# A decoder block on one core: attention and its output projection in one block of code, the projection's chunks in the order 2 3 0 1 6 4 5 7

## Chip, cores and metric

One core of a Trainium2 chip runs the whole kernel. The metric is the device time of one execution in microseconds (us). The kernel before took 1774.89 us (median of three runs, 1772.11 to 1775.58).

## What is computed

A decoder block for 1024 tokens of width 1024. The part that matters here is the attention branch and its output projection:

```
u = rms_norm(x, g_mix)
xr, gr, q, k, v, fl, m_lru, m_attn = split(u @ w_in)
y_lru  = (rg_lru(conv(xr)) * gelu(gr)) @ w_lru_out
o      = forgetting_attention(q, k, v, log_sigmoid(fl + b_forget))   # 8 heads of 128
y_attn = o @ w_attn_out
x = x + (sigmoid(m_lru) * y_lru + sigmoid(m_attn) * y_attn) @ w_out
x = x + hierarchical_moe(rms_norm(x, g_ffn), ...)
return rms_norm(x, g_final)
```

## The kernel before

The program is a row of nine stages (`write`): input norm, first value products, halved input products, LRU values, LRU output projection (`branch_out(0)`), attention (`attention`), attention output projection (`branch_out(1)`), merge projection with routing, experts. Each stage is a block with one instruction stream for each engine. `stage` ends each with a clearing of the stage's semaphores and a barrier of all engines, so no engine starts a stage before all have finished the last one.

All large products are made of float32r matmuls in three parts. An operand is split into a high part (ScalarE, ACT below, copies it to float32r) and a low part (VectorE, DVE below, subtracts that copy from the original); a product is high times high, high times low and low times high. `product` (L204) does this for one 128-row output tile of 1024 tokens: for each of the 8 chunks k of the inner dimension it issues six matmuls of 512 columns, 48 in all. Its argument `chunks_in` makes TensorE (PE) wait for each chunk's low part first.

**Attention.** Each of 8 heads goes through 8 score tiles of 128 queries, from the longest to the shortest: scores on PE (L1395), bias and minimum on DVE (L1492), exponent on ACT (L1444), turn on PE (L1404), high and low part of the turned tile on ACT and DVE (L1438, L1467), and, for each half of the queries, the product with the values on PE (`values`, L1419), which counts up `pv_mm`. The second half of the queries (g = 1, values product over 8 key blocks) comes first, then the first half (g = 0, 4 key blocks). DVE multiplies each half by the inverse sums (`output`, L1476), and SyncE (SP) stores it to `o_d` in DRAM (`store`, L1323). Result chunk k is head k: `o_d[k]`, 128 rows by 1024 tokens. The last `values` of the last head is the 16th, and so is its `output`.

**Between the two stages.** At the end of `attention`, SP issues the loads of chunks 0 to 3 from `o_d` into the four staging tiles `ao_in0` to `ao_in3` (L1359), behind the store of head 7's second half and ahead of the store of head 7's first half. SP's queue is in program order: every wait in it holds what stands behind it.

**Output projection.** `branch_out(1)` has chunks 4 to 7 loaded by SP into the same four staging tiles (L1148), each once the low part of the chunk that was there is made. ACT copies each chunk's high part to `uh` (L1187), DVE makes the low part in `ul` (L1205), PE runs `product` for four tile columns in each of two passes (L213). In the first of the eight products PE waits chunk by chunk. DVE gates each product with `ao_sg` (L1223), adds it to `mix` (L1226), and the result is split again (L1192, L1211). SP's loads of `ao_sg` (L1153) stand behind the chunk loads, ACT's split of the second weight block (L193) behind the eight chunk copies. The weights of the first pass are loaded long before.

The memory of `uh` and `ul` overlays that of attention: chunks 0 and 1 of `uh` lie where the first half's turned tiles (`at_pth0`) are, chunks 2 to 5 on the second half's (`at_pth1`), 6 and 7 on `at_ptl0`; chunks 0 to 3 of `ul` lie on `at_ptl1`. The staging tiles overlay the query and key tile of even heads.

Of the kernel before, what the change touches and what calls it, by code (L numbers as in the profile page):

```python
# [21 lines left out]


# [3 lines left out]
F32 = mybir.dt.float32  # L27
# [12 lines left out]
NH = 8  # L40
# [20 lines left out]
BANKS = 6  # L61
VALUE_USE = (0, 0, 1 + D // WB, 1 + D // WB)
# [7 lines left out]
SLOTS = (NE + MAXX) * BLK  # L70

# [30 lines left out]
class Kernel:  # L102
# [101 lines left out]
    def product(self, pe, ps, s, c, chunks_in=None, by_half=False):  # L204

        wh, wl = (w[s][:, :, c * P:(c + 1) * P] for w in (self.w_h, self.w_l))
        for half, k in ((half, k) for half in range(2 if by_half else 1) for k in range(KD)):
            if chunks_in is not None and half == (1 if by_half else 0):
                pe.wait_ge(chunks_in, k + 1)
            for w, u, first, last in ((wh, self.uh, k == 0, False), (wh, self.ul, False, False),  # L210
                                      (wl, self.uh, False, k == KD - 1)):
# [896 lines left out]
    def branch_out(self, branch):  # L1108
# [22 lines left out]
        in_hi, in_lo, own = (self.sem(f"{tag}_{n}") for n in ("hi", "split", "own"))  # L1131
        mix_hi, mix_lo = self.sem(f"{tag}_mix_hi"), self.sem(f"{tag}_mix_lo")
        both = [(s, c) for s in range(2) for c in range(2)]
        source = lambda k: k_.mix[:, k, :] if branch == 0 else stage[k % 4][:, :]
        new = slice(HALF if branch == 0 else 0, T)

        with nc.Block() as block:
            @block.sync
            def _(sp):
                if branch == 0:  # L1140
                    for q in range(4):
                        sp.wait_ge(k_.quad_stored[q], 16 * k_.quads_until(NBLOCKS))
# [7 lines left out]
                def gates(i):  # L1150
                    for s, c in both:
                        sp.wait_ge(gated[s][c], i)
                        sp.dma_start(sg[s][c][:, :], k_.sig_d[branch, 4 * i + 2 * s + c]).then_inc(loaded[s][c], 16)  # L1153
                with sp.Fori(0, n_pairs - 1) as i:
                    gates(i)
                    for s in range(2):
                        k_.load_block(sp, s, p0 + i + 1, k_.w_block(weights, WB * (2 + s) + 2 * WB * i))
                gates(n_pairs - 1)
                if branch == 0:

                    for c in range(2):
                        sp.wait_ge(k_.v_stored[c], 32 * D // WB * NT // 4)
                    sp.wait_ge(k_.bias_stored, 16)
                    for c in range(2):
                        if c == 0:
                            k_.load_head_qk(sp, 0, c)
                            k_.load_head_bias(sp, 0, c)
                        k_.load_head_v(sp, 0, c)
                for s in range(2):
                    k_.load_block(sp, s, p0 + n_pairs, k_.w_block(following, WB * s))  # L1170

            @block.tensor
            def _(pe):
                with pe.Fori(0, n_pairs) as i:
                    for s, c in both:
                        if c == 0:
                            pe.wait_ge(k_.w_lo[s], p0 + i + 1)
                        pe.wait_ge(gated[s][c], i)
                        k_.product(pe, k_.ps[2 * s + c], s, c, in_lo if (s, c) == (0, 0) else None, branch == 0 and (s, c) == (0, 0))\
                            .then_inc((k_.w_first, k_.w_used)[c][s], 1)  # L1180

            @block.scalar
            def _(act):
# [4 lines left out]
                def mixed_high(i, s, c):  # L1188
                    if branch == 1 and (i, s, c) != (n_pairs - 1, 1, 1):
                        n = 4 * i + 2 * s + c  # L1190
                        act.wait_ge(gated[s][c], i + 1)
                        act.activation(k_.mix_h[:, n, :], k_.mix[:, n, :], ACT.Copy).then_inc(mix_hi, 1)  # L1192
                for i in range(n_pairs):
                    k_.split_hi(act, 1, p0 + i)
                    for c in range(2):
                        mixed_high(i, 0, c)
                    k_.split_hi(act, 0, p0 + i + 1)
                    for c in range(2):
                        mixed_high(i, 1, c)

            @block.vector
            def _(dve):
                for k in range(KD):
                    dve.wait_ge(in_hi, k + 1)
                    dve.tensor_tensor(k_.ul[:, k, new], source(k)[:, new], k_.uh[:, k, new].bitcast(F32),  # L1205
                                      ALU.subtract).then_inc(in_lo, 1)
                def mixed_low(i, s, c):
                    if branch == 1 and (i, s, c) != (n_pairs - 1, 1, 1):
                        n = 4 * i + 2 * s + c
                        dve.wait_ge(mix_hi, n + 1)  # L1210
                        dve.tensor_tensor(k_.mix_l[:, n, :], k_.mix[:, n, :], k_.mix_h[:, n, :].bitcast(F32),  # L1211
                                          ALU.subtract).then_inc(mix_lo, 1)
                for i in range(n_pairs):
                    k_.split_lo(dve, 1, p0 + i)
                    for s, c in both:
                        dve.wait_ge((k_.w_first, k_.w_used)[c][s], p0 + i + 1)
                        dve.wait_ge(loaded[s][c], 16 * (i + 1))
                        mix = k_.mix[:, bass.ds(4 * i + 2 * s + c, 1), :].rearrange("p a t -> p (a t)")
                        if branch == 0:
                            dve.tensor_tensor(mix, k_.ps[2 * s + c][:, :], sg[s][c][:, :], ALU.mult)\  # L1220
                                .then_inc(gated[s][c], 1)
                        else:
                            dve.tensor_tensor(sg[s][c][:, :], k_.ps[2 * s + c][:, :], sg[s][c][:, :], ALU.mult)\  # L1223
                                .then_inc(own, 1)
                            dve.wait_ge(own, 4 * i + 2 * s + c + 1)
                            dve.tensor_tensor(mix, mix, sg[s][c][:, :], ALU.add).then_inc(gated[s][c], 1)  # L1226
                        mixed_low(i, s, c)
                        if (s, c) == (0, 1):
                            k_.split_lo(dve, 0, p0 + i + 1)
# [18 lines left out]
    def load_head_v(self, eng, i, c):  # L1248
        for part in range(2):
            eng.dma_start(self.at_v[c][:, part, :, :].bitcast(F32),  # L1250
                          self.v_d[i, part, :, :, c * HD:(c + 1) * HD]).then_inc(self.v_in[c], 16)

    def attention(self):
# [23 lines left out]
        inv_stored, inv_in = ([sem(f"at_inv_{n}{g}") for g in range(2)] for n in ("stored", "in"))  # L1277
        turns, tiles = NH // 2, 2 * NT
# [35 lines left out]
        with nc.Block() as block:  # L1314
            @block.sync
            def _(sp):
                def load_v(i, c):
                    sp.wait_ge(pv_mm, 4 * i - 2 + 2 * c)
                    k_.load_head_v(sp, i, c)

                def store(i, c, g):
                    sp.wait_ge(o_out, 4 * i + 2 * c + 2 - g)
                    sp.dma_start(k_.o_d[2 * i + c][:, g * HALF:(g + 1) * HALF], o_sb[g][:, :]).then_inc(stored[g], 16)  # L1323

                def inverses(i, c, g):
                    sp.wait_ge(inverted, tiles * i + NT * c + 8 - 4 * g)
                    rows = k_.inv_d[4 * i + 2 * c + g]
                    sp.dma_start(rows, inv[c][:, 4 * g:4 * g + 4]).then_inc(inv_stored[g], 16)
# [1107 lines left out]
```

## Time and profile before

| what | number |
|---|---|
| median of the runs | 1774.89 us |
| profiled execution, its own time | 1770.09 us |
| its span | 1768.5 us |
| PE busy | 1655.6 us (94%) |
| DVE busy | 1203.1 us (68%) |
| ACT busy | 886.5 us (50%) |
| POOL busy | 137.7 us (8%) |
| mean granted clock of PE | 0.977 |

The profiled execution's own time is 1.6 us more than its span, and lies 4.8 us under the median. Busy shares are means over all stages. The change touches the stretch from about 909 to 931 us, where attention ends and the output projection starts; the projection as a whole runs until about 1010 us. The timeline gives each instruction's start and, in square brackets, how long its engine was idle before it and what ended that. SPq marks DMA issues on SP's queue; the time of such a row is that of the issue, not of the transfer.

### The profile page before, as it was taken

How to read it: one execution, taken by the hardware profiler on the slowest of the kernel's cores; microseconds unless marked ns; L12 is line 12 of the kernel's file. 1: busy time of each engine (PE TensorE's matmuls, PEld its weight loads, DVE VectorE, ACT ScalarE, POOL GpSimd, SP SyncE). 2: the span in 40 equal slices, each digit the busy share in tenths (PEclk: the TensorE clock that was granted, in tenths of full speed). 3: DMA queues.
4: the chain of work that ended last, by engine and by line, in shares of the span. 5: the costliest groups of instructions: out<-in, count | busy, mean ns of one | idle time of the engine just before them, and what ended most of it. 6: DMA issues, size and time to landing. Idle time of an engine off the chain costs nothing. (4 is left out here: it accounts for less than half of the span.)

```text
span 1768.5 us, 22877 instructions
## 1 busy us (share of the span) xinstructions
PE 1655.6 (94%) x8336; PEld 1323.0 (75%) x8336; DVE 1203.1 (68%) x1441; ACT 886.5 (50%) x995; POOL 137.7 (8%) x187
## 2 busy tenths in 40 slices
PE   6999999999999999989989999599999999999991
PEld 5888888888888898878868798566677777777760
DVE  5877776643644662276764425679988888888886
ACT  6343343333455341065652102267777777777762
POOL 1000000000000000021100000100000000000015
PEclk9999999999999999999999999799999999999995
DMA  4254453342323233567862231499999999999977
GB/s 168 84 166 157 155 176 98 101 137 89 95 83 90 78 113 102 202 210 247 238 204 110 98 111 49 168 390 393 395 399 392 398 393 399 392 398 391 398 281 284
DMA packets 181078, 390.58 MB, mean 221 GB/s; under 512 B 15680, under 2 KB 91600, under 8 KB 179984
## 3 DMA queue, kind: packets, MB, share of 16 engines
q1 hardware_dynamic: 166880, 330.62, 51.7%
q0 software_dynamic: 8384, 29.63, 5.4%
q10 hardware_dynamic: 5744, 29.40, 4.6%
q8 instruction: 43, 0.70, 0.2%
q14 instruction: 27, 0.22, 0.0%
HBM read 322.15 MB, written 67.46 MB: 220 GB/s over the span
## 5 line engine op out<-in xcount | busy, mean ns | idle before, releaser
L1914 DVE TENSOR_TENSOR e_l<-e_raw,e_h 128x2048 fp32r<-128x2048 f32 x192 | 439.1, 2290 | 65.5 <-ACT e_h L1908 65.1
L1908 ACT ACTIVATE e_h<-e_raw 128x2048 fp32r<-128x2048 f32 x192 | 367.8, 1917 | 85.4 <-PE ps L1943 50.3
L1930 PE MATMUL ps<-e_h,e_xth 128*96 128x512 f32 x512 | 205.2, 401 | 6.2 <-DVE e_l L1914 3.0
L1930 PE MATMUL ps<-e_h,e_xtl 128*96 128x512 f32 x512 | 202.7, 396 | 0.0
L1930 PE MATMUL ps<-e_l,e_xth 128*96 128x512 f32 x512 | 201.9, 394 | 0.0
L213 PE MATMUL ps<-uh,w_h 128*128 128x512 f32 x512 | 162.0, 393 | 9.8 <-DVE ul L1205 5.5
L213 PE MATMUL ps<-ul,w_h 128*128 128x512 f32 x512 | 161.3, 391 | 0.0
L213 PE MATMUL ps<-uh,w_l 128*128 128x512 f32 x512 | 161.2, 391 | 0.0
L213 PEld LDWEIGHTS ps<-uh,w_h 128*128 128x128 f32 x512 | 96.6, 189 | 31.2 <-issue 9.9
L1930 PEld LDWEIGHTS ps<-e_h,e_xth 128*96 128x96 f32 x512 | 83.0, 162 | 46.4 <-issue 7.3
L213 PEld LDWEIGHTS ps<-ul,w_h 128*128 128x128 f32 x512 | 96.8, 189 | 20.3
L213 PEld LDWEIGHTS ps<-uh,w_l 128*128 128x128 f32 x512 | 96.7, 189 | 20.4
L1930 PEld LDWEIGHTS ps<-e_h,e_xtl 128*96 128x96 f32 x512 | 83.1, 162 | 36.2
L1930 PEld LDWEIGHTS ps<-e_l,e_xth 128*96 128x96 f32 x512 | 83.4, 163 | 32.0
L818 DVE TENSOR_TENSOR wn_stl<-wn_stl,ps 128x512 f32<-128x512 f32 x112 | 76.7, 685 | 44.7 <-PE ps L764 38.9
L193 ACT ACTIVATE w_h<-w_raw 128x2048 fp32r<-128x2048 f32 x22 | 42.0, 1909 | 87.7 <-DMA w_raw<-w_lru_out 49.1
L1943 PE MATMUL ps<-e_h,e_hth 128*96 128x512 f32 x256 | 82.6, 404 | 2.1 <-DVE e_htl L2064 2.1
L1943 PE MATMUL ps<-e_l,e_hth 128*96 128x512 f32 x256 | 80.6, 396 | 0.0
L1943 PE MATMUL ps<-e_h,e_htl 128*96 128x512 f32 x256 | 80.2, 394 | 0.0
L197 DVE TENSOR_TENSOR w_l<-w_raw,w_h 128x2048 fp32r<-128x2048 f32 x22 | 50.4, 2290 | 41.7 <-ACT w_h L193 41.7
L1995 POOL DMA_INDIRECT e_xg<-xn_d,slots_i x30 | 41.3, 1376 | 474.8 <-PE ps L2006 474.8
L225 PE MATMUL ps<-w_h,uh 128*128 128x256 f32 x256 | 73.7, 288 | 4.7 <-PEq L178 2.6
(685 smaller groups left out, 3405.2 us busy)
## 6 DMA issues: line engine op xcount, KB each, us to landing
e_raw<-w_exp_gate SPq DMA_DIRECT2D x64, 1024.0 KB, 19.7
e_raw<-w_exp_up SPq DMA_DIRECT2D x64, 1024.0 KB, 19.5
e_raw<-w_exp_down SPq DMA_DIRECT2D x64, 1024.0 KB, 19.0
wn_raw<-w_in SPq DMA_DIRECT2D x32, 512.0 KB, 5.0
w_raw<-w_in SPq DMA_DIRECT2D x12, 1024.0 KB, 5.3
at_qk<-qk_d ACTq DMA_DIRECT2D x6, 2048.0 KB, 9.7
y_d<-e_y ACTq DMA_DIRECT2D x32, 384.0 KB, 6.4
y_d<-zeros POOLq DMA_DIRECT2D x22, 384.0 KB, 3.9
```

Source lines behind the costliest of these rows:

```text
L193: act.activation(self.w_h[s][:, :, :], self.w_raw[s][:, :, :], ACT.Copy).then_inc(self.w_hi[s], 1)
L197: dve.tensor_tensor(self.w_l[s][:, :, :], self.w_raw[s][:, :, :], self.w_h[s][:, :, :].bitcast(F32), ALU.subtract).then_inc(self.w_lo[s], 1)
L213: mm = pe.matmul(ps[:, h * HALF:(h + 1) * HALF], w[:, k, :], u[:, k, h * HALF:(h + 1) * HALF], start=first, stop=last)
L225: mm = pe.matmul(ps, u[:, k, rows], w[s][:, k, :], start=first, stop=last)
L818: dve.tensor_tensor(out, part, bank(n, name), ALU.add).then_inc(added, 1)
L1908: act.activation(self.e_h[m % SPLIT][:, :, :], self.e_raw[slot][:, :, :], ACT.Copy).then_inc(self.e_hi[m % SPLIT], 1)
L1914: dve.tensor_tensor(self.e_l[slot][:, :, :], self.e_raw[slot][:, :, :], self.e_h[m % SPLIT][:, :, :].bitcast(F32), ALU.subtract).then_inc( ...
L1930: mm = pe.matmul(ps, x[:, k, :], w[:, k, :], start=first and first_piece, stop=last and last_piece)
L1943: mm = pe.matmul(ps[:, c * HALF:(c + 1) * HALF], x[:, at, :], w[:, 2 * k + c, :], start=first, stop=last)
L1995: pool.indirect_dma_start(out=xg[b][:, :], out_offset=None, in_=k_.xn_d, in_offset=bass.IndirectOffsetOnAxis(ap=slots, axis=0)).then_inc(g ...
```

## The change

`attention` and `branch_out` no longer open a block; each returns its five instruction streams (`Programs`). `run` opens one block and writes the streams of several stages one behind the other. The LRU output projection still stands alone (`lru_out`), attention and its output projection stand in one block (`attention_out`), with no clearing of semaphores and no barrier between them. The eight chunk splits are written by two new helpers, in the order `O_ORDER`, with waits of their own on `pv_mm`. DVE's splits of the first two chunks (2 and 3) stand ahead of the last `output` of attention. The first product of the projection takes its chunks in the same order, and so do SP's second four loads, whose position behind the last store is as it was. The rest of the diff is indentation.

```diff
+O_ORDER = (2, 3, 0, 1, 6, 4, 5, 7)
...
-    def product(self, pe, ps, s, c, chunks_in=None, by_half=False):
+    def product(self, pe, ps, s, c, chunks_in=None, by_half=False, order=range(KD)):
...
-        for half, k in ((half, k) for half in range(2 if by_half else 1) for k in range(KD)):
+        for half, n, k in ((half, n, k) for half in range(2 if by_half else 1) for n, k in enumerate(order)):
             if chunks_in is not None and half == (1 if by_half else 0):
-                pe.wait_ge(chunks_in, k + 1)
+                pe.wait_ge(chunks_in, n + 1)
...
                 else:
-                    for k in range(4, KD):
-                        for g in range(2):
-                            sp.wait_ge(k_.o_stored[g], 16 * (k + 1))
-                        sp.wait_ge(in_lo, k - 3)
-                        sp.dma_start(stage[k % 4][:, :], k_.o_d[k]).then_inc(in_loaded[k % 4], 16)
...
+                for k in O_ORDER[4:]:
+                    for g in range(2):
+                        sp.wait_ge(k_.o_stored[g], 16 * (k + 1))
+                    sp.wait_ge(in_lo, O_ORDER.index(k - 4) + 1)
+                    sp.dma_start(stage[k % 4][:, :], k_.o_d[k]).then_inc(in_loaded[k % 4], 16)
...
-                for k in range(KD):
-                    if branch == 1:
-                        act.wait_ge(in_loaded[k % 4], 16 * (k // 4 + 1))
-                    act.activation(k_.uh[:, k, new], source(k)[:, new], ACT.Copy).then_inc(in_hi, 1)
...
+            for n in range(KD):
+                if branch == 1:
+                    k_.o_high(act, n)
...
+            if branch == 1:
+                for n in range(2, KD):
+                    k_.o_low(dve, n)
...
+    def o_high(self, act, n):
+        k = O_ORDER[n]
+        act.wait_ge(self.o_in[k % 4], 16 * (k // 4 + 1))
+        act.wait_ge(self.pv_mm, 2 * NH - (n < 2))
+        act.activation(self.uh[:, k, :], self.o_stage[k % 4][:, :], ACT.Copy).then_inc(self.o_hi, 1)
+
+    def o_low(self, dve, n):
+        k = O_ORDER[n]
+        dve.wait_ge(self.o_hi, n + 1)
+        dve.tensor_tensor(self.ul[:, k, :], self.o_stage[k % 4][:, :], self.uh[:, k, :].bitcast(F32),
+                          ALU.subtract).then_inc(self.o_lo, 1)
...
+            for n in range(tiles, tiles + VALUES - 1):
+                step(turns - 1, n)
+            for n in range(2):
+                k_.o_low(dve, n)
+            step(turns - 1, tiles + VALUES - 1)
...
+    def lru_out(self):
+        self.run(self.branch_out(0))
+
+    def attention_out(self):
+        self.run(self.attention(), self.branch_out(1))
...
-                             (self.branch_out, 0), (self.attention,), (self.branch_out, 1), (self.project_route,),
+                             (self.lru_out,), (self.attention_out,), (self.project_route,),
```

On DVE, where attention ends, the order before (`at_o0` is the last output, of head 7's first half; `ul` is a chunk's low part):

```order
L1467 TENSOR_TENSOR at_ptl0_6915<-ps3,at_pth0_6913 128x128
L1476 TENSOR_TENSOR at_o0_6910<-ps3,at_invb0_6928 128x512
L1314 UNCONDITIONAL_BRANCH
L1201 UNCONDITIONAL_BRANCH
L1205 TENSOR_TENSOR ul_67<-ao_in0_6537,uh_66 128x1024
L1205 TENSOR_TENSOR ul_67<-ao_in1_6538,uh_66 128x1024
```

and now:

```order
L1487 TENSOR_TENSOR at_ptl0_6918<-ps3,at_pth0_6916 128x128
L1275 TENSOR_TENSOR ul_67<-ao_in2_6539,uh_66 128x1024
L1275 TENSOR_TENSOR ul_67<-ao_in3_6540,uh_66 128x1024
L1496 TENSOR_TENSOR at_o0_6913<-ps3,at_invb0_6931 128x512
L1275 TENSOR_TENSOR ul_67<-ao_in0_6537,uh_66 128x1024
L1275 TENSOR_TENSOR ul_67<-ao_in1_6538,uh_66 128x1024
```

The last output moved behind the low parts of the chunks in staging tiles 2 and 3, which before came third and fourth.

On SP's queue at the same place, before (the store of `at_o1` is that of head 7's second half, the store of `at_o0` that of its first half):

```order
L1323 DMA o_d<-at_o1_6911 128x512
L1359 DMA ao_in0_6537<-o_d 128x1024
L1359 DMA ao_in1_6538<-o_d 128x1024
L1359 DMA ao_in2_6539<-o_d 128x1024
L1359 DMA ao_in3_6540<-o_d 128x1024
L1323 DMA o_d<-at_o0_6910 128x512
L1314 UNCONDITIONAL_BRANCH
L1138 UNCONDITIONAL_BRANCH
L1148 DMA ao_in0_6537<-o_d 128x1024
L1148 DMA ao_in1_6538<-o_d 128x1024
L1148 DMA ao_in2_6539<-o_d 128x1024
L1148 DMA ao_in3_6540<-o_d 128x1024
```

and now:

```order
L1347 DMA o_d<-at_o1_6914 128x512
L1383 DMA ao_in0_6537<-o_d 128x1024
L1383 DMA ao_in1_6538<-o_d 128x1024
L1383 DMA ao_in2_6539<-o_d 128x1024
L1383 DMA ao_in3_6540<-o_d 128x1024
L1347 DMA o_d<-at_o0_6913 128x512
L1153 DMA ao_in2_6539<-o_d 128x1024
L1153 DMA ao_in0_6537<-o_d 128x1024
L1153 DMA ao_in1_6538<-o_d 128x1024
L1153 DMA ao_in3_6540<-o_d 128x1024
```

The first four loads and the store behind them stand where they stood, in the order 0 1 2 3; the second four come as chunks 6, 4, 5, 7, behind that store, and the block's end between them is gone.

## Rows read from the trace of the kernel before

**Rows 1.** The waits of PE between 903 and 930 us (waits in us, times, longest).
```profile
PE ps L213 <- DVE ul L1205: 5.5, 3, 4.9
PE ps L1419 <- DVE at_ptl L1467: 1.3, 1, 1.3
```

**Rows 2.** Timeline of PE: start us, us, instruction, count, idle before and what ended it.
```profile
911.69 0.27 PE L1419 MATMUL ps<-at_pth,at_v 128*128 128x128 f32 x1
916.88 1.19 PE L213 MATMUL ps<-uh,w_h 128*128 128x512 f32 x2 [4.92 <-DVE ul L1205]
...
919.58 0.73 PE L213 MATMUL ps<-uh,w_h 128*128 128x512 f32 x2
...
928.96 0.73 PE L213 MATMUL ps<-uh,w_h 128*128 128x512 f32 x2 [0.27 <-DVE ul L1205]
...
930.46 0.63 PE L213 MATMUL ps<-uh,w_h 128*128 128x512 f32 x2
...
941.36 0.62 PE L213 MATMUL ps<-uh,w_h 128*128 128x512 f32 x2
```

**Rows 3.** Timeline of ACT, first set of chunks, and the last chunk.
```profile
908.57 0.28 ACT L1438 ACTIVATE at_pth<-ps 128x128 fp32r<-128x128 f32 x1 [4.21 <-PE ps L1404]
914.42 1.06 ACT L1187 ACTIVATE uh<-ao_in 128x1024 fp32r<-128x1024 f32 x1 [5.58 <-DMA ao_in<-o_d]
915.69 1.06 ACT L1187 ACTIVATE uh<-ao_in 128x1024 fp32r<-128x1024 f32 x1 [0.21 <-DMA ao_in<-o_d]
917.21 1.06 ACT L1187 ACTIVATE uh<-ao_in 128x1024 fp32r<-128x1024 f32 x1 [0.46 <-DMA ao_in<-o_d]
918.55 1.06 ACT L1187 ACTIVATE uh<-ao_in 128x1024 fp32r<-128x1024 f32 x1 [0.28 <-DMA ao_in<-o_d]
921.23 1.06 ACT L1187 ACTIVATE uh<-ao_in 128x1024 fp32r<-128x1024 f32 x1 [1.61 <-DMA ao_in<-o_d]
...
926.59 1.06 ACT L1187 ACTIVATE uh<-ao_in 128x1024 fp32r<-128x1024 f32 x1 [0.88 <-DMA ao_in<-o_d]
```

**Rows 4.** Timeline of SP's queue over the same stretch; the time is that of the issue.
```profile
909.61 0.32 SPq L1323 DMA_DIRECT2D o_d<-at_o  x1
910.04 1.81 SPq L1359 DMA_DIRECT2D ao_in<-o_d  x4
913.17 0.32 SPq L1323 DMA_DIRECT2D o_d<-at_o  x1
916.83 4.44 SPq L1148 DMA_DIRECT2D ao_in<-o_d  x4
```

**Rows 5.** DMA issues between 909.5 and 910.3 us: size of each, us from issue to landing.
```profile
ao_in<-o_d SPq DMA_DIRECT2D x1, 512.0 KB, 4.4
o_d<-at_o SPq DMA_DIRECT2D x1, 256.0 KB, 2.3
```

**Rows 6.** Timeline of DVE: the last output, the first two low parts, the last one.
```profile
912.10 1.05 DVE L1476 TENSOR_TENSOR at_o<-ps,at_invb 128x512 f32<-128x512 f32 x1 [2.31 <-PE ps L1419]
915.51 2.50 DVE L1205 TENSOR_TENSOR ul<-ao_in,uh 128x1024 fp32r<-128x1024 f32 x2 [2.37 <-ACT uh L1187]
...
927.68 1.23 DVE L1205 TENSOR_TENSOR ul<-ao_in,uh 128x1024 fp32r<-128x1024 f32 x1 [0.71 <-ACT uh L1187]
```

**Rows 7.** Stretches: busy us (count) of PE, PEld, DVE, ACT, POOL; clock, DMA share, GB/s.
```profile
914.00:916.00 2.00, 0.00 (x0) 0.00 (x0) 0.49 (x1) 1.36 (x2) 0.00 (x0) 1.00 1.00 375
916.00:918.00 2.00, 1.12 (x3) 0.95 (x4) 1.96 (x2) 1.54 (x2) 0.00 (x0) 0.59 1.04 398
918.00:920.00 2.00, 2.00 (x7) 1.57 (x6) 1.59 (x3) 1.33 (x2) 0.00 (x0) 0.55 1.12 302
920.00:922.00 2.00, 2.00 (x11) 1.62 (x10) 0.87 (x1) 0.77 (x1) 0.00 (x0) 1.00 0.93 283
```

**Rows 8.** Two shorter gaps of PE at other stages, and the stretches around them.
```profile
755.22 0.99 PE L1395 MATMUL ps<-at_qk 128*128 128x512 f32 x3 [2.23 <-PEq L178]
...
755.00:760.00 5.00, 4.78 (x15) 3.99 (x16) 1.57 (x3) 2.48 (x3) 1.42 (x4) 0.66 1.09 420
...
1010.05 0.36 PE L225 MATMUL ps<-w_h,mix_h 128*128 128x256 f32 x1 [3.25 <-PEq L178]
...
1008.00:1012.00 4.00, 1.95 (x16) 1.98 (x17) 2.17 (x3) 1.18 (x2) 1.43 (x11) 1.00 0.92 301
```

More of the change, by code:

```diff
@@ L24 @@
+from collections import namedtuple
 import concourse.bass as bass
@@ L70 @@
 SLOTS = (NE + MAXX) * BLK
+Programs = namedtuple("Programs", "sync gpsimd tensor scalar vector")
 class Map:
@@ L1130, in branch_out @@
         in_loaded = k_.o_in
-        in_hi, in_lo, own = (self.sem(f"{tag}_{n}") for n in ("hi", "split", "own"))
+        in_hi, in_lo = (self.sem("lo_hi"), self.sem("lo_split")) if branch == 0 else (k_.o_hi, k_.o_lo)
+        own = self.sem(f"{tag}_own")
         mix_hi, mix_lo = self.sem(f"{tag}_mix_hi"), self.sem(f"{tag}_mix_lo")
         both = [(s, c) for s in range(2) for c in range(2)]
-        source = lambda k: k_.mix[:, k, :] if branch == 0 else stage[k % 4][:, :]
-        new = slice(HALF if branch == 0 else 0, T)
@@ new lines, in tensor @@
+        def tensor(pe):
+            with pe.Fori(0, n_pairs) as i:
+                for s, c in both:
+                    if c == 0:
+                        pe.wait_ge(k_.w_lo[s], p0 + i + 1)
+                    pe.wait_ge(gated[s][c], i)
+                    k_.product(pe, k_.ps[2 * s + c], s, c, in_lo if (s, c) == (0, 0) else None, branch == 0 and (s, c) == (0, 0),
+                                  O_ORDER if branch == 1 and (s, c) == (0, 0) else range(KD))\
+                        .then_inc((k_.w_first, k_.w_used)[c][s], 1)
@@ new lines, in scalar, with mixed_high @@
+        def scalar(act):
+            for n in range(KD):
+                if branch == 1:
+                    k_.o_high(act, n)
+                else:
+                    act.activation(k_.uh[:, n, new], k_.mix[:, n, new], ACT.Copy).then_inc(in_hi, 1)
+            def mixed_high(i, s, c):
+                if branch == 1 and (i, s, c) != (n_pairs - 1, 1, 1):
+                    n = 4 * i + 2 * s + c
+                    act.wait_ge(gated[s][c], i + 1)
+                    act.activation(k_.mix_h[:, n, :], k_.mix[:, n, :], ACT.Copy).then_inc(mix_hi, 1)
+            for i in range(n_pairs):
+                k_.split_hi(act, 1, p0 + i)
+                for c in range(2):
+                    mixed_high(i, 0, c)
+                k_.split_hi(act, 0, p0 + i + 1)
+                for c in range(2):
+                    mixed_high(i, 1, c)
@@ L1213, in _, with mixed_low @@
[L1213 to L1229, printed above, removed]
+            def mixed_low(i, s, c):
+                if branch == 1 and (i, s, c) != (n_pairs - 1, 1, 1):
+                    n = 4 * i + 2 * s + c
+                    dve.wait_ge(mix_hi, n + 1)
+                    dve.tensor_tensor(k_.mix_l[:, n, :], k_.mix[:, n, :], k_.mix_h[:, n, :].bitcast(F32),
+                                      ALU.subtract).then_inc(mix_lo, 1)
@@ new lines, in scalar, with high, exponent, step @@
+        def scalar(act):
+            def high(i, n):
+                for st in of_tile[n]:
+                    act.wait_ge(t_mm, len(parts) * i + st + 1)
+                    later(act, pv_mm, 4 * i + n // 4 - 1)
+                    act.activation(piece(pt_h, st), turned(st).rearrange("p (k q) -> p k q", q=P),
+                                   ACT.Copy).then_inc(hi, 1)
+            def exponent(i, n):
+                keys = (block_of(n) + 1) * P
+                act.wait_ge(least, tiles * i + n + 1)
+                act.activation(sb[n % NT][:, 0:keys], sb[n % NT][:, 0:keys], ACT.Exp, scale=-1.0,
+                               bias=small[:, n % 2, 0:1], accum_out=small[:, n % 2, 1:2]).then_inc(exped, 1)
+            def step(i, n):
+                if n < tiles:
+                    exponent(i, n)
+                if n % NT == NT - 1 and n < tiles and (type(i) is not int or i < turns - 1):
+                    k_.load_head_qk(act, i + 1, n // NT)
+                if tile := back(i, n, AHEAD - 1):
+                    high(*tile)
+            for n in range(tiles):
+                step(0, n)
+            with act.Fori(1, turns - 1) as i:
+                for n in range(tiles):
+                    step(i, n)
+            for n in range(tiles + VALUES + 1):
+                step(turns - 1, n)
```

444 lines of the change are left out of this document (216 added, 228 removed).

## The prediction

> **What bounds the kernel now.** The page says that PE is busy 94% of the span, so a change can only matter where PE stands still, or where it makes PE stand still. I therefore read PE's waits around the stage boundary first [rows 1]: in the first product of the projection PE waits 5.5 us for DVE's low parts, 4.9 us of it in one piece. The timeline of PE [rows 2] places it: the last values matmul starts at 911.69 and ends at 911.96, the first matmul of the projection starts at 916.88. From 930.46 the second product runs without a gap: 24 pairs of matmuls in 941.36 - 930.46 = 10.90 us, 1.36 us for the six of one chunk. So what counts is one moment: when the last chunk of the first product can start (now 928.96). All later work of this projection hangs on PE from there on.
>
> Next I ask what holds DVE. ACT's timeline [rows 3] shows that ACT has nothing left of attention after 908.85 and that each chunk copy starts when a DMA lands: 914.42, 915.69, 917.21, 918.55, 921.23, and so on to 926.59. SP's queue [rows 4] and the landings [rows 5] say why: the first four loads are issued from 910.04, right behind the store of 909.61, and the first lands 4.4 us later, at 914.4. That is the start of ACT to a tenth of a microsecond. The barrier between the stages therefore costs nothing now: DVE's last output ends at 913.15 [rows 6], all engines are through before 914.42, and what they wait for then is data.
>
> **The change part by part.** Removing the block's end, the clearing and the barrier: 0 us. The cover is the 4.4 us of the first load. If it were gone (loads issued earlier), DVE's output up to 913.15 would be next.
>
> *The order 2 3 0 1 against the order of the loads.* SP still loads 0 1 2 3. ACT now waits for chunk 2 first, which lands third, at 917.21 and not at 914.42; chunk 3 lands at 918.55. The new waits on `pv_mm` are met by then (the last values matmul ends at 911.96), so they cost nothing. Step by step:
> - high part of chunk 2: 917.21 to 918.27 (1.06 us, rows 3); low part, 0.03 us behind, 1.23 us: 918.30 to 919.53 [rows 6]. PE follows DVE by 0.14 us (first low part ends at 916.74, PE starts at 916.88), so it starts at about 919.7 and not at 916.88.
> - chunk 3: high part 918.55 to 919.61, low part 919.64 to 920.87.
> - the last output of attention, which now stands behind these two on DVE: 1.05 us, 920.90 to 921.95. It was done at 913.15. This is the costly part: 8.8 us later.
> - low parts of chunks 0 and 1, long in: 921.97 to 923.20 and to 924.43.
>
> *SP's queue.* The store of the last output waits for it, and the second four loads stand behind the store. The store is issued at 921.97 (now 913.17), chunk 6 at 922.40 (0.43 us behind, as 910.04 stands behind 909.61, rows 4), chunk 4 at 923.3 when chunk 0's low part is made, chunk 5 at 924.5, and chunk 7 at 924.9: it also needs the store's landing, 2.3 us [rows 5], 924.3. Before, these four were issued from 916.83 to 920.95. So the first of the second set is 5.6 us later, the last one 4.0 us later.
>
> *The landings.* Chunk 6 lands at 922.40 + 4.4 = 926.8; both sets took 4.4 us for their first (910.04 to 914.42, 916.83 to 921.23). From the first to the last landing the first set took 4.13 us, with its issues spread over 1.4 us, the second 5.36 us, with issues over 4.1 us [rows 3, 4]. Here the issues spread over 2.5 us. I take a point in between, in proportion to the spread: 4.6 us, so chunk 7 lands at 931.4. The ends are 930.9 and 932.2; kept for the range.
>
> *The end.* From the last landing to PE's last chunk now takes 928.96 - 926.59 = 2.37 us. The same from 931.4 gives 933.8, which is 4.8 us later than 928.96. From the ends: 4.3 to 5.6 us. A lower bound holds even if the loads went faster than any seen in pace: the store lands at 924.3, a load takes 4.4 us, plus 2.37 us gives 931.1, that is 2.1 us later.
>
> *PE's clock.* After the 4.9 us gap PE was granted the low level, 1.2 GHz: 0.59 and 0.55 in two stretches of 2 us, then 1.00 [rows 7]. The first six matmuls took 919.58 - 916.88 = 2.70 us instead of 1.36. The gap is now 7.7 us, so this comes again, from 919.7 on. It costs nothing in the sum: PE has done chunks 2, 3, 0, 1 by about 926.9 and then waits for chunk 6 until 929.2 anyway. That second gap of about 2.3 us is new. Whether it lowers the clock again rows don't settle: after a gap of 2.23 us the clock was 0.66 over 5 us, after one of 3.25 us it stayed at 1.00 [rows 8]. I count 0 for it, and 1.7 us (half of the 3.4 us that 0.66 over 5 us stands for) at the upper end.
>
> *The rest.* The loads of `ao_sg` stand behind the chunk loads and now come from about 925.4; the first has until the end of the first product, near 935.2, and lands behind chunk 7 some 1.3 us, the step between the first set's landings. The second weight block's split on ACT and DVE follows the last chunk as before and is needed one product later still, 10.9 us. Both hidden. Nothing behind 930 has a due time that stays where it was, so the delay passes to the end in full.
>
> **Sum:** +4.8 us, from 2.1 to 5.6 + 1.7 = 7.3 us. Against the profiled execution's own 1770.09 us this gives 1774.9; the median of the runs lies 4.8 us above that execution, so I put the forecast at 1774.89 + 4.8 = 1779.7 us, and my own range for this case is 1777.0 to 1782.2.
>
> **The rivals.**
>
> *A. The gap lowers the clock again.* PE waits at about 926.9, as above, and runs chunks 6, 4, 5 at half speed; the last ones then follow from work and not from landings: +6.0 to 7.3 us, 1781.5. For it speaks the 2.23 us gap [rows 8], against it the 3.25 us gap. The Trainium skill, "TensorE: Matmul & The Clock Gate", section "HAM oscillation — how this bites in real kernels", describes this: waits for DMA between tiles let the clock fall again and again. By that rule the time would be this rival's and not the sum's; rows 7 agree for a long gap, rows 8 go both ways for a short one.
>
> *B. The delay is mostly hidden.* The engines of the DMA were at a share of 0.93 to 1.12 through this stretch [rows 7]. If the second set, with the queue empty before it, lands at the pace that the store's landing allows, only the 2.1 us of the lower bound are left, 1777.0. Against it: the first set, with only a store before it, took 4.13 us from first to last.
>
> *C. Faster.* If chunks 2 and 3 were in before PE is through with values, the design pays. The place is the landing of chunk 3: the whole chain behind it (two splits' ends, output, store, loads) moves with it one to one, so the +4.8 of 918.55 becomes nothing at 918.55 - 4.8 = 913.8. Below that it gains: with both low parts made before 912, the output is at 912.10 to 913.15 as now, chunk 6 goes at 913.6, chunk 7 lands 4.4 + 4.6 us later at 922.6, PE's last chunk starts at 925.0, 4.0 us earlier: 1770.9. For it: ACT is idle from 908.85, and the second half's tiles are free by then. Against it: the loads are issued from 910.04 on and land one after the other, third and fourth being those that are wanted first. The Trainium skill, "DMA: Bandwidth & Descriptors", section "Queues, rings and completion order", says that descriptors are consumed in ring order but that completion need not be in the order of issue; here the four landed in order, 1.3 to 1.5 us apart, and even all at 914.4 would not suffice.
>
> **How the numbers follow.** A measurement of this kernel can tell about 0.2% from no change, 3.5 us. Chances: the forecast 0.50, A 0.18, B 0.22, C 0.10. The runs of before spread over 3.5 us, so the forecast of +4.8 comes out above 3.5 in about three of four cases: slower 0.50 x 0.74 + 0.18 x 0.95 + 0.22 x 0.1 = 0.56; C gives faster, 0.08 of its 0.10; the rest is within 0.2%: 0.36. The range takes in the whole of the forecast's own and A's, and reaches below 1777.0 for B with the spread of the runs: 1774.5 to 1782.5.
>
> **What would show it.** In the profile after: the first chunk copy on ACT about 2.8 us later, ended by a DMA; the last output on DVE behind two low parts, 8.8 us later; the last store at about 922 and the second loads from 922.4; PE's gap about 7.7 us, a second gap of about 2.3 us before chunk 6, the last chunk of the first product at about 933.8. The attention before 909 and everything behind the projection unchanged in length. The prediction is wrong if the loads of chunks 2 and 3 land before 914, if the store is issued long before 922, or if a later stage takes the delay up.

## The result, and the profile after

The changed kernel takes 1778.91 us (median of 20 runs, 1774.31 to 1784.31), the kernel before 1773.35 us (20 runs, 1771.94 to 1778.26). The ratio is 1.0028, 95% interval [1.0021, 1.0036]: 5.0 us slower, with 3.7 to 6.4 us. The profiled execution has a span of 1772.7 us against 1768.5.

All the work was there before: the page counts 8336 matmuls in both. So I read the stretch around the old stage boundary again. First PE: its timeline, with the idle time and what ended it in brackets. Answers to [rows 2].

```profile
910.54 0.27 PE L1441 MATMUL ps<-at_pth,at_v 128*128 128x128 f32 x1
918.26 1.19 PE L220 MATMUL ps<-uh,w_h 128*128 128x512 f32 x2 [7.45 <-DVE ul L1275]
...
920.96 1.05 PE L220 MATMUL ps<-uh,w_h 128*128 128x512 f32 x2
...
926.91 0.73 PE L220 MATMUL ps<-uh,w_h 128*128 128x512 f32 x2
...
929.17 0.73 PE L220 MATMUL ps<-uh,w_h 128*128 128x512 f32 x2 [0.61 <-DVE ul L1275]
...
932.05 0.62 PE L220 MATMUL ps<-uh,w_h 128*128 128x512 f32 x2
...
933.41 0.62 PE L220 MATMUL ps<-uh,w_h 128*128 128x512 f32 x2
```

The last values matmul ends at 910.81 here (911.96 before: attention happened to go 1.2 us faster in this execution). So absolute times of two traces are not to be compared; I count from the end of that matmul. Then the first product starts at 7.45 us (4.92 before) and the second, at 933.41, at 22.60 us (930.46 - 911.96 = 18.50 before). **4.1 us of the loss stand in this one stretch.** Below, "S" is this distance, from the last values matmul's end to the second product's start. Both ends are single rows, and the first product's work lies wholly in between.

Then who keeps PE waiting: DVE, and behind it SP's queue and ACT. Answers to [rows 6], [rows 4] and [rows 3].

```profile
916.89 2.48 DVE L1275 TENSOR_TENSOR ul<-ao_in,uh 128x1024 fp32r<-128x1024 f32 x2 [8.26 <-ACT uh L1270]
919.29 1.09 DVE L1496 TENSOR_TENSOR at_o<-ps,at_invb 128x512 f32<-128x512 f32 x1
920.28 2.37 DVE L1275 TENSOR_TENSOR ul<-ao_in,uh 128x1024 fp32r<-128x1024 f32 x2
```

```profile
908.88 1.80 SPq L1383 DMA_DIRECT2D ao_in<-o_d  x4
920.41 0.32 SPq L1347 DMA_DIRECT2D o_d<-at_o  x1
920.85 2.69 SPq L1153 DMA_DIRECT2D ao_in<-o_d  x4
```

```profile
915.80 1.06 ACT L1270 ACTIVATE uh<-ao_in 128x1024 fp32r<-128x1024 f32 x1 [8.11 <-DMA ao_in<-o_d]
917.06 2.95 ACT L1270 ACTIVATE uh<-ao_in 128x1024 fp32r<-128x1024 f32 x3 [0.20 <-DMA ao_in<-o_d]
924.54 1.06 ACT L1270 ACTIVATE uh<-ao_in 128x1024 fp32r<-128x1024 f32 x1 [4.53 <-DMA ao_in<-o_d]
926.80 1.06 ACT L1270 ACTIVATE uh<-ao_in 128x1024 fp32r<-128x1024 f32 x1 [1.21 <-DMA ao_in<-o_d]
928.12 1.06 ACT L1270 ACTIVATE uh<-ao_in 128x1024 fp32r<-128x1024 f32 x1 [0.25 <-DMA ao_in<-o_d]
929.37 1.06 ACT L1270 ACTIVATE uh<-ao_in 128x1024 fp32r<-128x1024 f32 x1 [0.20 <-DMA ao_in<-o_d]
```

Chunk 2's copy starts at 4.99 us, where chunk 0's stood at 2.46. The last output begins at 8.5 us, not at 0.14, since it stands behind two low parts. The last store goes at 9.60 instead of 1.21, and the second loads at 10.04 instead of 4.87. The last chunk lands at 18.56 instead of 14.63.

And PE's clock, as stretches (the columns of rows 7):

```profile
918.00:920.00 2.00, 1.74 (x4) 1.48 (x5) 1.97 (x3) 2.00 (x3) 0.00 (x0) 0.50 0.04 8
920.00:922.00 2.00, 2.00 (x6) 1.51 (x6) 2.00 (x3) 0.01 (x1) 0.00 (x0) 0.50 0.47 145
922.00:924.00 2.00, 2.00 (x7) 1.51 (x6) 0.65 (x1) 0.00 (x0) 0.00 (x0) 0.50 0.85 270
924.00:926.00 2.00, 2.00 (x10) 1.60 (x9) 0.37 (x1) 1.06 (x1) 0.00 (x0) 0.91 0.89 334
```

The low level lasts 6 us of work here, against 2.7 before, and the DMA engines lie idle (share 0.04) while the loads wait behind the store.

One more thing these rows show: the chunk that PE last had to wait for is chunk 4 (929.17, idle for 0.61 us), not chunk 7. Chunk 7's low part was ready at 931.68 and PE took it up at 932.05, straight from chunk 5. In the kernel before, PE did wait for its last chunk (0.27 us, [rows 2]).

The rest of the difference between the two spans (4.2 us in all) is give and take between two executions. From the second product to the merge projection both have 79.6 to 79.7 us; from there to the experts' first matmul it is 138.6 us after and 137.1 before, a stretch in which the other profiled runs have 137.2 to 141.1 whatever the edit. This is why the experiments are judged by S first and by the time of the whole second. But S comes from one profiled execution of each kernel, and a second one of the changed kernel (e11) differs by 0.8 us. Differences in S below about 1 us are therefore not shown by S alone, and the whole time cannot show them either.

### The profile page after: what moved, and what is told of

Same layout as the page of the kernel before. It is cut to its first block and busy times, and to the rows that moved or that the text cites. A ratio compares the mean times of both kernels' runs of the same rounds, so it can differ in the third digit from the quotient of the medians.

```text
span 1772.7 us, 22862 instructions
## 1 busy us (share of the span) xinstructions
PE 1658.2 (94%) x8336; PEld 1324.5 (75%) x8336; DVE 1203.1 (68%) x1441; ACT 886.7 (50%) x995; POOL 137.7 (8%) x187
```

## The experiments

The theory: the last landing of the second loads sets the end, and two things made it late: first loads that arrive in another order than they are used, and an output, hence a store, hence a queue of loads, behind two splits. Rivals: the one block itself, the low clock, or something outside. The section "One rule" below shows that "the last landing" is only nearly right.

**e1: loads in the order 2 3 0 1.**

```diff
-            for r in range(4):
+            for r in O_ORDER[:4]:
                 sp.dma_start(k_.o_stage[r][:, :], k_.o_d[r]).then_inc(k_.o_in[r], 16)
```

> The changed kernel, but SP issues the first four loads in the order 2 3 0 1. Theory (landings set the end): chunk 3 lands 2.8 us earlier, the last output, the store and the second loads follow one to one, so of the about 4.1 us that PE's first product ends late 2.8 us are gone: 1.0 to 1.6 us over the kernel before. Rival (the block's fusion itself costs, or something outside this stretch): still 4 to 5 us over.

Measured: ratio 1.0012 [0.9999, 1.0025], S 21.87 us, 3.4 over before. The store went at 7.37 us (9.60 in the changed kernel) and the last chunk landed at 16.44 instead of 18.56: this part of the chain moved by 2.2 us and 2.1 us. But PE did not follow. Its rows, from the gap on:

```profile
927.82 0.73 PE L220 MATMUL ps<-uh,w_h 128*128 128x512 f32 x2 [2.07 <-DVE ul L1275]
928.39 0.67 PE L220 MATMUL ps<-ul,w_h 128*128 128x512 f32 x2
928.86 1.06 PE L220 MATMUL ps<-uh,w_l 128*128 128x512 f32 x2
929.72 1.06 PE L220 MATMUL ps<-uh,w_h 128*128 128x512 f32 x2
930.57 1.06 PE L220 MATMUL ps<-ul,w_h 128*128 128x512 f32 x2
931.42 1.01 PE L220 MATMUL ps<-uh,w_l 128*128 128x512 f32 x2
932.27 0.62 PE L220 MATMUL ps<-uh,w_h 128*128 128x512 f32 x2
```

Having waited 2.07 us for chunk 6, PE fell to the low clock (a pair in 0.85 us instead of 0.45), four pairs long: 1.6 us. So the expected size was missed by the clock, the mechanism of rival A; the expectation had left it out. Without these 1.6 us S would have been about 20.3 (an estimate from these rows), 1.8 over before and still a little above the 1.0 to 1.6 that were expected. As it is, S is 0.73 us below the changed kernel's, no more than two executions of one kernel differ by.

**e2: the last output ahead of the splits.**

```diff
-            for n in range(tiles, tiles + VALUES - 1):
+            for n in range(tiles, tiles + VALUES):
                 step(turns - 1, n)
             for n in range(2):
                 k_.o_low(dve, n)
-            step(turns - 1, tiles + VALUES - 1)
```

> The changed kernel, but DVE's last output stands ahead of the low parts of chunks 2 and 3 again. Theory: store and second loads are no longer held; chunk 6 is issued when chunk 2's low part is made (about 919.6 on the time axis of the kernel before), chunks 4, 5, 7 up to 923.8, the first product ends about 2.4 us late: 2.0 to 2.8 us over before. Rival (the order is the whole cost, the output behind it nothing): 4 us over.

Measured: ratio 1.0015 [1.0001, 1.0029], S 21.74. The store is back at 1.21 us. Chunk 6's load is issued at 7.66 instead of 10.04, as expected, but lands 5.3 us later (3.7 in the changed kernel), and the last chunk lands at 17.79: only 0.8 us of the 2.4 are kept. Between theory (2.0 to 2.8 over) and rival (4): 3.2 over, and S alone cannot tell it from the changed kernel (0.86 us less).

**e3: both edits.**

> Both edits together: loads in the order 2 3 0 1 and the last output ahead of the splits. Theory: chunk copy, PE's start and the second loads are back where they were in the kernel before, 0 us (-0.4 to +0.4); the one block gains nothing while the loads are issued at 910. Rival (fusion costs by itself): over 2 us slower than before.

Measured: S 19.54, so 3.06 of the 4.10 us are gone. The two edits alone took off 0.73 and 0.86; together they take off more than the sum. The rows suggest why, each alone leaving the other wait, or the clock, as the bound; with one profile each, that the two add up to more is not shown. It is not back at 18.50: chunk 4 and chunk 5 landed 3.26 us apart (11.02 and 14.28), where the others of this set were 1.3 and 1.4 us apart. The 1.04 us that remain lie outside the expected 0.4. The ratio of the whole, 1.0015 [1.0002, 1.0027], allows 0.4 to 4.8 us over before: it does not separate theory from rival, nor e3 from e1 or e2.

A part of what remains may come from the queue's own order. The loads go 6, 4, 5, 7, and chunk 4's goes into the tile of chunk 0, whose low part is made third. The tile of chunk 3 is free after the second low part, at 6.2 us, but chunk 7's load for it stands last. So in e3 the second load of the set is issued at 7.91 us (before, with 4, 5, 6, 7: 6.13). No run tried 6, 7, 4, 5.

**e4: only the one block.** `O_ORDER` is `tuple(range(KD))`, the last output first as in e2, and the copies wait for all 16 values products.

> The changed kernel with the natural order 0 to 7 everywhere and the last output first: only the one block without a barrier is left of the change. Theory: 0 us against before, since the first load's landing at 914.4 hides the barrier. Rival (the block's end did cost something): faster by 0.5 us or more, with the first chunk copy on ACT earlier.

Measured: ratio 1.0006 [0.9994, 1.0019], S 18.41. The first copy of ACT in its trace:

```profile
916.57 1.06 ACT L1270 ACTIVATE uh<-ao_in 128x1024 fp32r<-128x1024 f32 x1 [6.36 <-DMA ao_in<-o_d]
```

It waits for the DMA as before (and came at 3.25 us, not earlier than 2.46). So here the data is what ACT waits for, with or without a barrier, and no cost of the one block shows; the whole time allows 1.1 us less to 3.4 us more than before. This run is also the clearest sign of the cause: with the order and the place of the output undone, all of the 4.1 us are gone from S, and the interval of the whole, [0.9994, 1.0019], lies below that of the changed kernel, [1.0021, 1.0036]. The rival that the one block itself costs the 4 us falls.

**e5: chunk 6's load ahead of the last store.** The changed kernel, with chunk 6's load taken out of `branch_out` and, in `sync` of attention:

```diff
+            for g in range(2):
+                sp.wait_ge(stored[g], 16 * 7)
+            sp.wait_ge(k_.o_lo, 1)
+            sp.dma_start(k_.o_stage[2][:, :], k_.o_d[6]).then_inc(k_.o_in[2], 16)
             store(turns - 1, 1, 0)
```

> The changed kernel, but SP issues chunk 6's load ahead of the last store. Measured from the end of the last values matmul to the start of the second product (18.50 us before, 22.60 us after). Theory (second loads held behind the store): chunk 6 lands 2.5 us earlier, chunks 4, 5, 7 a little, 21.2 to 21.6 us. Rival (the store's place on the queue costs nothing, all is the order): 22.6 us.

Measured: ratio 1.0024 [1.0011, 1.0037], S 22.30, nearer to the rival. The load went 2.4 us earlier (7.63) but landed at 12.80, 0.9 us earlier; the other three were issued from 11.31 and the last landed at 18.36. S is 0.3 us less than in the changed kernel, which is within what two executions differ by. PE's last wait was before chunk 5, which had landed at 17.08 us; chunk 6 was not what it lacked.

**e6: no idle time for PE in the first gap.** 32 matmuls, each of 512 columns, whose result nobody uses:

```diff
             steps(pe, step)
+            filler = k_.w_h[0][:, 0:2, :].rearrange("p k n -> p (k n)")
+            for _ in range(32):
+                pe.matmul(k_.ps[1][:, 0:HALF], k_.w_h[0][:, 0, 0:P], filler, start=True, stop=True)
```

> The changed kernel with 32 extra matmuls of 512 columns on PE (weights already in, into a free PSUM tile, results unused) between the last values and the first product, so that PE is not idle in the gap. Theory (landings set the end, the low clock is covered): from the last values to the second product 22.3 to 22.6 us, as after; the wait before chunk 6 shows instead. Rival (the 6 us at the low clock are the price): about 3 us less, 19.6 us.

Measured: ratio 1.0032 [1.0020, 1.0045], S 25.82, worse than both. The rows of PE:

```profile
919.08 0.70 PE L220 MATMUL ps<-uh,w_h 128*128 128x512 f32 x2 [0.69 <-DVE ul L1275]
...
927.57 0.73 PE L220 MATMUL ps<-uh,w_h 128*128 128x512 f32 x2 [2.18 <-DVE ul L1275]
...
930.10 1.22 PE L220 MATMUL ps<-uh,w_h 128*128 128x512 f32 x2 [0.65 <-DVE ul L1275]
931.12 1.05 PE L220 MATMUL ps<-ul,w_h 128*128 128x512 f32 x2
...
933.67 1.05 PE L220 MATMUL ps<-ul,w_h 128*128 128x512 f32 x2
934.53 1.05 PE L220 MATMUL ps<-uh,w_l 128*128 128x512 f32 x2
```

The first product now starts at the full clock, so the edit did what it was for. It brought nothing there: PE runs into a wait of 2.18 us for chunk 6 instead, and then falls to the low clock with the last chunks, where nothing covers it. The rival (3 us gained) is refuted; the theory's number is missed by 3.2 us. Of these, 0.7 us are landings (the last at 19.25 instead of 18.56 us); the other 2.5 us are the low clock behind the second gap.

**e7 and e8: the first loads 15 us earlier.** In the kernel before and in the changed one, the first four loads go right behind head 6, ahead of `head(turns - 1, 1)` (shown for e8; in e7 the loop stays `range(4)`):

```diff
-            for c in range(2):
-                head(turns - 1, c, last=True)
+            head(turns - 1, 0, last=True)
             sp.wait_ge(least, tiles * (turns - 1) + NT)
             for g in range(2):
                 sp.wait_ge(stored[g], 16 * 4)
-            for r in range(4):
+            for r in O_ORDER[:4]:
                 sp.dma_start(k_.o_stage[r][:, :], k_.o_d[r]).then_inc(k_.o_in[r], 16)
+            head(turns - 1, 1, last=True)
             store(turns - 1, 1, 0)
```

> The kernel before, but SP issues the first four loads about 20 us earlier, ahead of the last head's stores. The landing no longer hides the barrier. Theory: all engines have to pass the last output at 1.2 us after the last values and the barrier; ACT's first chunk copy starts about 3 us after the values instead of 2.5, second product at 18 to 19 us (18.50 before): no gain. Rival (landing of the first set was the bound also past the barrier): 16.5 us or less.

> The changed kernel with the same early loads, in the order 2 3 0 1. Theory: chunks 2 and 3 are split during the last values product, PE goes on without a gap, store and second loads at 1.5 to 4.5 us, second product at 14.2 to 16.0 us (18.50 before, 22.60 after), so 2.5 to 4.3 us faster than before. Rival (the order or the one block cost by themselves): over 18.5 us.

Measured, e7: ratio 1.0007 [0.9999, 1.0016], S 18.77. With the data long in, ACT is held by the block's end, as its row says (PEq is PE's sequencer; the last output, too, came 0.85 us late):

```profile
914.86 3.90 ACT L1187 ACTIVATE uh<-ao_in 128x1024 fp32r<-128x1024 f32 x4 [6.88 <-PEq L178]
```

Measured, e8: ratio 0.9988 [0.9975, 1.0001], S 16.35, 2.15 us under before. PE goes on into the projection without a gap. So the one block and the order 2 3 0 1 need the early loads: the early loads alone show no gain (e7), and the change alone costs 4.1 us of S. Over the whole the gain of e8 is not quite shown; its interval allows 0.2 us more to 4.4 us less than before. S misses my 14.2 to 16.0 by a little, by the clock (see the rule below) and by the output, which DVE's rows show late:

```profile
909.09 2.35 DVE L1275 TENSOR_TENSOR ul<-ao_in,uh 128x1024 fp32r<-128x1024 f32 x2
912.62 1.08 DVE L1496 TENSOR_TENSOR at_o<-ps,at_invb 128x512 f32<-128x512 f32 x1 [1.18 <-DMA at_invb<-inv_d]
```

It waits for its inverse sums. SP's queue shows where their round trip through DRAM (store to `inv_d`, broadcast to `at_invb`) was held:

```profile
894.80 1.87 SPq L1382 DMA_DIRECT2D ao_in<-o_d  x4
896.71 0.56 SPq L1352 DMA_DIRECT2D inv_d<-at_inv  x1
904.40 0.32 SPq L1355 DMA_DIRECT2D at_invb<-inv_d  x1
904.76 0.43 SPq L1347 DMA_DIRECT2D o_d<-at_o  x1
905.24 0.43 SPq L1352 DMA_DIRECT2D inv_d<-at_inv  x1
909.11 0.32 SPq L1355 DMA_DIRECT2D at_invb<-inv_d  x1
```

The sums of the second half, behind 2 MB of early loads, take 7.7 us from store to broadcast. The broadcast of the first half's sums comes later on the same queue, and so leaves only 2.3 us before the values' end. In the kernel before that last round trip took 1.4 us (904.03 to 905.43) and its broadcast left 6.5 us ahead. This was not expected.

**e9: e8 with e5's edit.**

> The changed kernel with early first loads (2 3 0 1) and chunk 6's load ahead of the last store. Theory: chunk 6 is issued at about 0 us after the last values and lands at 3.7 to 4.4, the gap of PE before it goes; chunk 4 lands at 7.3 to 8.3, second product at 14.0 to 14.9 us, or up to 15.7 if the clock falls once. Rival (PE's rate or the low clock and not the landings are left as the bound): 16 us, as with early loads alone.

Measured: 1771.36 us against 1774.20, ratio 0.9979 [0.9967, 0.9992]: faster than the kernel before by 3.7 us (1.4 to 5.9), the best of all. S is 16.92, no better than e8's and over the range that I gave. The output came late again (1.66 us of idle time of DVE, ended by the DMA of `at_invb`), and chunks 4 and 5 landed 3.9 us apart. The low clock did not occur in this stretch. By S alone it gains 1.6 us, so a part of the 3.7 is the luck of its runs or lies elsewhere; e8 and e9 are not told apart by their intervals. Neither side of the expectation holds: the number is nearer to the rival's 16 us, but no low clock did it. PE waited 2.23 us for chunk 5, so the landings were the bound, and they came late.

**e10: early loads, natural order** (e4 with the early loads).

> One block, natural order 0 to 7, last output first, first four loads early: the order 2 3 0 1 is undone. Theory: chunk 0 cannot be split before the last values product, PE starts 2.5 us after it, but the store leaves at 1.2 us and the second loads at 2.5 to 6.2 us: second product at 14.7 to 16 us, no later than with the order 2 3 0 1. Rival (the order is what makes early loads pay): 17.5 us or more.

Measured: ratio 0.9993 [0.9983, 1.0003], S 17.46, as good as the rival's 17.5. PE starts at 3.72 us and not 2.5, since the output, again late for its inverse sums, holds the low parts. It starts at the low clock and never waits again: its eight chunks took 13.7 us instead of the 10.9 us of the full clock. S is 1.1 us above e8's. That the order 2 3 0 1 is worth this much with early loads is likely but not shown: two executions of one kernel differ by 0.8 us, and the whole times of e8 and e10 do not differ clearly.

**e11: the changed kernel once more.**

> The changed kernel once more, one look. Theory: from the last values to the second product 22 to 23 us again, with the same order of events; only the stretches at the low clock may lie differently. Rival (the 22.6 us was chance): under 21 us.

Measured: S 23.39, slightly over my bound, same order of events: gap of 8.17 us, store at 10.31, last landing at 19.35. The size repeats to 0.8 us, and 4.1 is the lower of two values.

**e12: first loads behind the last broadcast of inverse sums.** Issued 6.1 us before the values' end, so that they cannot delay it; chunk 6's load as in e5; on DVE the last output between the low parts of chunks 2 and 3:

```diff
             for n in range(tiles, tiles + VALUES - 1):
                 step(turns - 1, n)
-            for n in range(2):
-                k_.o_low(dve, n)
+            k_.o_low(dve, 0)
             step(turns - 1, tiles + VALUES - 1)
+            k_.o_low(dve, 1)
```

> The changed kernel with the first four loads (2 3 0 1) issued right behind the last broadcast of inverse sums, about 4 us earlier than in the kernel before and not 15 us as in the last runs, chunk 6's load ahead of the last store, and the last output between the low parts of chunks 2 and 3. Theory (the very early loads delayed the inverse sums and with them the last output): the output is at 0.6 to 1.7 us after the last values, chunk 6 is issued at about 0.7 us, second product at 14.6 us (18.50 before, 16.92 with the very early loads); over the whole 3.5 to 4 us faster than before. Rival (the pace of the second loads is the bound whatever the output does): 16.5 us or more.

Measured: ratio 1.0000 [0.9988, 1.0012], S 16.69. The output is no longer delayed by the sums, but by chunk 2, which landed at -0.28 us, 5.8 us behind its issue; so the output began at 1.96 us and not at 0.6, the store went at 3.08 and the last chunk landed at 12.62. The rival's number was met. PE's first gap was only 2.18 us, and it fell to the low clock behind it. S is 1.8 us under before, the whole time is not; the interval allows a gain of 2.1 us at most. So a gain in S need not show in the whole.

**One rule over all runs.** The prediction took 2.37 us from the last landing to PE's last chunk; with the 1.36 us of that chunk, S should be the last landing plus 3.73 us. The last column names the last chunk of the first product before which PE was idle:

| kernel | last chunk lands, us | + 3.73 | S measured | difference | last wait before chunk |
|---|---|---|---|---|---|
| before | 14.63 | 18.36 | 18.50 | 0.1 | 7 |
| changed | 18.56 | 22.29 | 22.60 | 0.3 | 4 |
| e1 | 16.44 | 20.17 | 21.87 | 1.7 | 6 |
| e2 | 17.79 | 21.52 | 21.74 | 0.2 | 5 |
| e3 | 15.58 | 19.31 | 19.54 | 0.2 | 5 |
| e4 | 14.07 | 17.80 | 18.41 | 0.6 | none |
| e5 | 18.36 | 22.09 | 22.30 | 0.2 | 5 |
| e6 | 19.25 | 22.98 | 25.82 | 2.8 | 4 |
| e7 | 14.88 | 18.61 | 18.77 | 0.2 | none |
| e8 | 11.77 | 15.50 | 16.35 | 0.9 | 4 |
| e9 | 12.98 | 16.71 | 16.92 | 0.2 | 5 |
| e10 | 13.27 | 17.00 | 17.46 | 0.5 | none |
| e11 | 19.35 | 23.08 | 23.39 | 0.3 | 4 |
| e12 | 12.62 | 16.35 | 16.69 | 0.3 | 4 |

The three large differences, e1, e6 and e8, are those in which PE waited over 2 us for chunk 6 and fell to the low clock behind it.

The rule fits the others within 0.6 us, but only in the kernel before was the last landing itself what PE waited for. Where the column names another chunk, PE started that one 2.37 us after its landing (changed kernel: 15.99 + 2.37 = 18.36) and then ran without a gap. The chunks behind it landed about 1.3 us apart and PE takes 1.36 us for one, so the last landing plus 3.73 comes out nearly the same. In e4, e7 and e10 PE never waited after its first chunk: there S is set by when PE starts and by the low clock behind the first gap, which costs 1.8, 2.2 and 2.8 us against the 10.9 us of eight chunks at the full clock.

## Why the prediction was right

**The first copy.** Forecast 2.8 us later, ended by a DMA; it is 2.5 later (4.99 against 2.46), ended by the DMA. Chunks 0 to 3 landed in the order of their issue, at 2.2, 3.7, 5.0 and 6.2 us.

**The output, the store, the second loads.** Forecast 8.8, 8.8 and 5.6 us later for the first of the second set; measured 8.3, 8.4 and 5.2. That this chain, together with the order of the first loads, is the cause is shown by e3 and e4: with both mended 3.1 of the 4.1 us go from S, with the natural order back all of them, and e4 also over the whole. How the loss divides between the two is not shown.

**The landings.** Chunk 6 landed 3.7 us after its issue, not 4.4; first to last took 4.8 us, not 4.6. The last landing came 3.9 us later than before, forecast 4.8. This is the term that was oversized, by 0.9 us: 0.4 from a chain that started less late, 0.7 from the faster first load, less 0.2 from the spread. From the last landing to PE's last chunk it took 2.68 us and not 2.37, because PE was still at work on the chunks before it; this made the end 0.3 later than the landings alone would have.

**The end.** Forecast +4.8 for PE's last chunk. Measured 932.05 - 910.81 = 21.24 against 17.00: +4.2 in the profile, +4.1 for S, +4.9 for S in e11, +5.0 (3.7 to 6.4) over all runs. That 4.8 stands so near to 5.0 is in part luck: the profile read for it gives 4.2. In absolute terms 1779.7 us were forecast and 1778.91 measured; the three runs that the forecast started from lay 1.5 us above the median of all twenty.

**The barrier at 0 us.** Right as far as the runs can tell: e4, and from the other side e7, where it shows once the data are early.

**The clock.** The count was right, its reasoning was wrong. I had PE finish chunks 2, 3, 0, 1 at about 14.9 us (the 6.9 us that the first four chunks took before, from 919.7, give 14.7) and then wait 2.3 us for chunk 6, with a chance of a second stretch at the low clock. Instead the low level lasted 6 us of work behind the 7.45 us gap, not 2.7; chunk 6 came early, and the two met almost exactly (926.91). So the slow start filled the gap that would have caused the next one. That the clock cost about nothing is luck, not insight. e6 shows the other branch: with a fast start the gap is there, and rival A's mechanism then costs about 2.5 us. The rule of the Trainium skill, "TensorE: Matmul & The Clock Gate", cited with rival A, agrees with e1, e6 and e8; e9, with a wait of 2.23 us and no fall, goes against it, and in the changed kernel itself it did not decide.

**Rivals.** B, mostly hidden: its bound of 2.1 us was not approached. C, faster if chunks 2 and 3 are in early: its condition was met in e8. A gain came in S, though 2.15 us and not 4.0; over the whole only e9, with one more edit, is clearly faster.

## What to carry to other kernels

Removing a barrier pays only where nothing else is awaited at it; look at what ended the idle time of the first instruction behind it, and make that early first. When the order in which chunks are used is changed, change the order of the loads with it, and ask of each instruction that is put ahead of another what the delayed one feeds: here one multiplication of 1 us on DVE held a store and four loads on SP's queue. And find the piece that the slow engine last waits for, not the one that comes last: it is that piece's arrival that a change has to move. An early load is not free either, since it stands ahead of small round trips on the same queue.

## What was not expected of the hardware

- A gap can be worth filling only if no other follows. After waits of 2.07, 2.18 and 2.32 us for one chunk (e1, e6, e8), and after the 2.18 us ahead of the first product in e12, PE fell to the low clock; after waits of 0.61 us (changed kernel) and of 2.23 us before chunk 5 (e9) it did not.
- How long the low level lasts behind a gap did not follow from the gap. Behind the first one, PE's pairs were slow for about 3.1 us after 2.18 us idle (e12), 2.7 us after 4.92 (before), 3.6 us after 5.17 (e1) and 6.1 us after 7.45 (changed kernel), but also for 6.0 us after 3.72 (e10) and 5.7 us after 4.54 (e3).
- The first load of the second set, 512 KB each time, took from 3.6 (e4, e6) to 5.8 us (e9) from issue to landing; in the kernel before it was 4.4 us. How far ahead of it the last store stands on the queue does not explain this. With the store 0.4 us ahead it took 3.6 to 4.5 us (changed kernel, e1, e6, e8, e11). Elsewhere it mostly took 4.6 to 5.8 us (e2, e3, e5, e7, e9, e10, e12), but in e4 and in the kernel before, with the store 4.2 and 3.7 us ahead, only 3.6 and 4.4 us.
- The last two loads of the set landed 1.25 to 1.37 us apart in every run except the kernel before (1.9). That pace is 512 KB in about 1.27 us, 413 GB/s, and the profile has the DMA engines full then (changed kernel, 928 to 930 us: share 1.04, 422 and 426 GB/s). Ahead of these two, most runs have one or two steps of 1.8 to 2.9 us, and two runs one of 3.3 (e3) and 3.9 us (e9), both between chunks 4 and 5. In e9's step the DMA engines were 77 to 95% busy (921 to 925 us, 250 to 381 GB/s) and moved about twice the 512 KB of one load, so other transfers went on meanwhile. What sets these steps stays open; no run was made for it.
- Small round trips through DRAM are held by large loads in front of them on the queue: 7.7 us from the store of 2 KB of inverse sums to their broadcast (e8).
